# Expert weights loaded by two engines, half of each partition's run apiece

## What is computed

```
def expert_choice_ffn(h, w_router, w_gate, w_up, w_down):
    cap = EC_CAPACITY_FACTOR * n // N_EXPERTS              # 32 tokens
    aff = softmax(h @ w_router)
    g, idx = lax.top_k(aff.transpose(0, 2, 1), cap)
    xs = h[idx]
    a = jnp.einsum('becd,edf->becf', xs, w_gate)
    u = jnp.einsum('becd,edf->becf', xs, w_up)
    y = jnp.einsum('becf,efd->becd', jax.nn.silu(a) * u, w_down)
    y = y * g[..., None]
    return scatter_add(y, idx)
```

## Time and profile before

| | |
|---|---|
| median of three runs | 2280.72 us |
| the three runs | 2279.51, 2280.72, 2283.62 us |
| span of the profiled execution | 2283.8 us |
| PE busy | 1954.9 us, 86% |
| DVE, ACT, POOL busy | 929.5, 684.9, 4.1 us |
| bytes moved by DMA | 606.56 MB |
| chain that ended last, by engine | PE 52%, DMA 28%, DVE 13%, ACT 6%, issue 2% |

### The profile page before, as it was taken

One profiled execution on the slowest core, in us unless ns is written; L12 is line 12 of the kernel. 1 busy time (PEld: TensorE's weight loads), 2 busy tenths in 40 slices (PEclk: granted clock), 3 DMA queues, 4 the chain that ended last, 5 costly groups with the idle time before them and its releaser, 6 DMA issues.

```text
span 2283.8 us, 30557 instructions
## 1 busy us (share of the span) xinstructions
PE 1954.9 (86%) x13502; PEld 1393.4 (61%) x13502; DVE 929.5 (41%) x1596; ACT 684.9 (30%) x1090; POOL 4.1 (0%) x11
## 2 busy tenths in 40 slices
PE   7999999889898999999999888878889976566666
PEld 5589999878776999866774332324256843232323
DVE  5776655667665665664441010101065511010101
ACT  5345544553424454544422100000034310000000
POOL 0000000000000000000000000000000000000000
PEclk9999999899999999999999999999999988788878
DMA  6664445441457445512226999999932689999998
GB/s 262 239 263 154 169 162 188 156 167 56 185 221 281 167 148 181 206 41 111 111 111 287 428 427 428 428 427 428 428 137 111 260 355 426 428 427 427 427 427 339
DMA packets 44788, 606.56 MB, mean 266 GB/s; under 512 B 5104, under 2 KB 5232, under 8 KB 6768
## 3 DMA queue, kind: packets, MB, share of 16 engines
q1 hardware_dynamic: 43488, 597.61, 64.3%
q0 software_dynamic: 880, 4.98, 0.7%
q10 hardware_dynamic: 288, 2.02, 0.2%
HBM read 603.54 MB, written 1.05 MB: 265 GB/s over the span
## 4 chain that ended last, share of the span: by engine, by line
PE 52%; DMA 28%; DVE 13%; ACT 6%; issue 2%; SPq 0%; DVEq 0%; ACTq 0%
PE ps L85 51%; DMA m_more<-moe_up 10%; DMA m_ring<-moe_up 5%; DMA m_ring<-moe_down 3%; DVE m_WL L94 2%; DMA m_moe_sc<-moe_gate 2%; DMA m_side_slot<-moe_down 2%; DMA m_more<-moe_down 2%; DMA m_more<-moe_gate 1%; DMA m_ring<-moe_gate 1%; ACT m_WH L91 1%; ACT m_mix_sc L91 1%; DVE m_od_low L100 1%; DMA m_ring<-ev_in 1%; PE ps L88 1%
## 5 line engine op out<-in xcount | busy, mean ns | idle before, releaser
L94 DVE TENSOR_TENSOR m_WL<-m_ring,m_WH 128x1024 fp32r<-128x1024 f32 (+1 forms) x277 | 330.0, 1202 | 262.6 <-ACT m_WH L91 261.8
L85 PE MATMUL ps<-m_more,m_moe_sc 128*32 128x256 f32 (+1 forms) x1648 | 317.4, 538 | 80.6 <-DMA m_more<-moe_up 51.7
L91 ACT ACTIVATE m_WH<-m_ring 128x1024 fp32r<-128x1024 f32 (+1 forms) x277 | 282.4, 1034 | 132.2 <-PE ps L85 120.8
L85 PE MATMUL ps<-m_ring,m_moe_sc 128*32 128x256 f32 (+1 forms) x1104 | 244.8, 549 | 57.2 <-DMA m_ring<-moe_gate 28.3
L85 PEld LDWEIGHTS ps<-m_more,m_moe_sc 128*32 128x32 f32 (+1 forms) x1648 | 119.0, 141 | 226.7 <-issue 115.0
L85 PE MATMUL ps<-m_nH,m_WH 128*128 128x256 f32 x936 | 234.5, 287 | 18.3 <-ACT m_WH L91 18.3
L85 PE MATMUL ps<-m_nL,m_WH 128*128 128x256 f32 x936 | 234.5, 288 | 9.1 <-DVE m_nL L100 8.9
L85 PEld LDWEIGHTS ps<-m_nH,m_WH 128*128 128x128 f32 x936 | 181.0, 193 | 22.0 <-ACT m_WH L91 20.1
L85 PEld LDWEIGHTS ps<-m_nL,m_WH 128*128 128x128 f32 x936 | 181.1, 193 | 12.7 <-DVE m_nL L100 11.9
L85 PEld LDWEIGHTS ps<-m_ring,m_moe_sc 128*32 128x32 f32 (+1 forms) x1104 | 89.0, 143 | 149.8 <-issue 76.4
L91 ACT ACTIVATE m_moe_sc<-ps 32x512 f32<-32x512 f32 (+3 forms) x86 | 40.1, 472 | 385.9 <-PE ps L85 374.6
(11 more groups left out here) (307 smaller groups left out, 3199.2 us busy)
## 6 DMA issues: line engine op xcount, KB each, us to landing
m_more<-moe_up SPq DMA_DIRECT2D x37, 2048.0 KB, 26.6
m_more<-moe_gate SPq DMA_DIRECT2D x33, 2048.0 KB, 26.7
m_more<-moe_down SPq DMA_DIRECT2D x29, 2048.0 KB, 23.6
m_ring<-moe_gate SPq DMA_DIRECT2D x26, 2048.0 KB, 25.0
m_ring<-moe_down SPq DMA_DIRECT2D x25, 2048.0 KB, 26.7
m_ring<-ada SPq DMA_DIRECT2D x24, 2048.0 KB, 7.5
m_ring<-moe_up SPq DMA_DIRECT2D x22, 2048.0 KB, 25.6
m_ring<-ffn_down SPq DMA_DIRECT2D x16, 1408.0 KB, 6.0
```

The costliest lines, as they stand in the source:

```text
L85: return Issued() if self.dry else self.e.matmul(out, lhsT, rhs, start=start, stop=stop, skip_group_check=skip)
L91: return Issued() if self.dry else self.e.activation(*a, **k)
L94: return Issued() if self.dry else self.e.tensor_tensor(*a)
```

## The change

For the expert matrices alone (`moe_gate`, `moe_up`, `moe_down`), SP loads the left 8 KB of each partition's 16 KB (`width = SLOT // 2`, column tiles 0 and 1 of the chunk), and POOL the right 8 KB (column tiles 2 and 3). POOL goes through the same list of chunks in the same order, with the same events before each, once per layer and after its own load of `poolA`. Its loads signal semaphores of their own (`right0` to `right8`), and PE waits for both signals of a chunk where it waited for one. All other loads are as before.

```diff
+EXPERTS = ("moe_gate", "moe_up", "moe_down")
...
                             c = cc[h * nj // 4]
-                            pe.wait_ge(*at(("landed", c)))
+                            pe.wait_ge(*at(("landed", c))).wait_ge(*at(("right landed", c)))
...
                         c = down[h * nj // 4]
-                        pe.wait_ge(*at(("landed", c)))
+                        pe.wait_ge(*at(("landed", c))).wait_ge(*at(("right landed", c)))
...
         def pool_program():
             landed = {n: count(n) for n in ("p_landed", "ctx_landed", "dft_landed", "pools_landed")}
+            right = [count(f"right{i}") for i in range(9)]
...
                 pool.dma_start(wk[:, :], dr["poolA"]).then_inc(*landed["pools_landed"].mark(("poolA landed", l), by=16))
+                for n, (name, idx, j0, m, kt, _, slot, before) in enumerate(W.chunks):
+                    if name not in EXPERTS or idx[0] != l:
+                        continue
+                    for event in before:
+                        pool.wait_ge(*at(event))
+                    pool.dma_start(slots[slot][:, SLOT // 2:SLOT], dr[name][l][idx[1]][j0 // 4][:, SLOT // 2:SLOT]).then_inc(
+                        *right[slot].mark(("right landed", n), by=16))
...
                 per, width = TILES.get(kt, 1), m * kt * 128
+                if name in EXPERTS:
+                    width = SLOT // 2
                 sp.dma_start(slots[slot][:, 0:width], w[j0 // per][:, 0:width]).then_inc(*landed[slot].mark(("landed", n), by=16))
```

## The result

The changed kernel takes 2299.65 us (2298.78 to 2301.84, four runs), the kernel before 2281.38 us in the same comparison: a ratio of **1.0075** (95% interval 1.0062 to 1.0089), 14 to 20 us slower. It was forecast as slower, at 2290 us in a range of 2279 to 2304. The direction and the main mechanism held. The size was nearly double the forecast.

The account below looks back on a forecast made before the run. The prediction took DMA bytes over rate in the two expert parts as the bound. Rows (+40 ns) and signal (+12 ns) over 174 loads gave +9.0 us, other terms zero: 2290 us, range 2279 to 2304.

Parts of the forecast that it names:

- What bounds the kernel: Both expert parts: DMA engines full, shares 1.00 and 0.99, so bytes divided by rate bound them; PE has slack.
- Two of the signs: Expert parts: PE's load waits grow as much as the parts, some 4.5 us each; clearly later rights would be wrong.
- Part 1: Expert loads: twice as many rows, of 8 KB, cost +40 to +91 ns per 2 MB load; +40 taken.
- Part 2: Expert loads: a second signal for each load costs +12 ns (0 to 25) on each DMA engine.
- Part 3: POOL's issue of right halves: they start 0.3 us later, hidden by over 20 us of queued loads; zero.
- Part 4: PE's second wait per expert chunk: 0 to 0.04 us each, hidden in PE's slack except 0.04 us at the last load.
- Part 5: SP's and POOL's queues in the expert parts: equal turns with 8 KB rows mean equal bytes; zero.
- The sum: Whole kernel: 174 loads at +52 ns give +9.0 us, so 2290 us; at most +116 ns a load, +20 us.
- Two queues filling each other's gaps: Rival, expert parts: alternating queues reach 436 GB/s, -90 ns a load, -16 us, 2265 us; chance 0.07.
- The small cost: Rival, expert rows: fixed cost smaller than read, under 26 ns a load, -4 to +4.5 us, about 2283 us; chance 0.18.
- The right half falling behind: Rival, ends of expert parts: POOL gets fewer turns, last chunks bunch, +12 us, 2302 us with the +9; chance 0.08.
- POOL's loads one after the other, or descriptors late all the way: Rival, expert parts: right halves go at 5.1 us a load for 4.91, +33 us, 2314 us; chance 0.09.

Follow-up runs that it names:

- e9: Kernel before, expert matrices laid out by halves, so SP's one 2 MB transfer with one signal moves two 8 KB rows per partition; ratio 1.0052.
- e8: e1 with both half transfers on the slot's one semaphore, so PE waits once per chunk; ratio 1.0054 against the kernel before.
- e1: The change, but SP issues both halves of every expert chunk on one queue, a signal each; 2300.65 us, ratio 1.0069.
- e5: The change, but the last expert of each layer is loaded whole by SP; ratio 1.0050 against the kernel before.
- e2: Against the change: whole 2 MB expert chunks in 16 KB rows, first of each matrix by SP, second by POOL; ratio 1.0040.
- e7: Against e2: all expert chunks whole by POOL, all other weights by SP; ratio 1.0083.
- e6: e2, but the last expert of each layer is loaded by SP alone; ratio 0.9999 against the kernel before.

## Why the prediction was right, and where it was off

**What bounds the kernel.** Right. The DMA share stayed full, the rate fell from 428 to 421 GB/s (423 was forecast), and both expert parts grew. All that was found to change lies in them, but for 0.7 us less in the mixer between. Two of the signs came out otherwise: PE's waits for loads grew by 2.3 us in the first window (39.2 for 36.9), less than the part, and by 9.8 us in the second, and in the second part the rights land clearly later than the lefts.

**Part 1, the rows: the right term, mis-sized.** The bounds were +40 and +91 ns a load and I took +40, from 310.6 ns a row in a lone load of POOL. Measured: +71 ns (e9), 174 x 71 = 12.4 us, against 12.6 us in the parts. The step that failed is the price of a row from a lone load, and of its two windows the lower one. In the same measure, busy share over rows, e9's stream gives 101.1% of 3200 us / 10274 rows = 314.9 ns a row. The 313.8 ns that I put aside as an edge effect was nearer. But the measure itself isn't good enough: 16 x 314.9 less 8 x 616.3 is +108 ns, where the bytes moved give +71. Shares of 100.4 and 101.1% can't be exact, and 1% of a load is 49 ns, most of the effect. So whether a lone row is really faster than one in a stream can't be told from these numbers.

The estimate from the Trainium skill ("DMA: Bandwidth & Descriptors", Why small descriptors are slow), 3.5 ns a row, is too small here as the whole fixed cost of a row: the three row lengths give 9 ns.

**Part 2, the second signal.** Forecast +12 ns a load, 2 us. e8 has two transfers and two signals a load where e9 has one of each, and the same rows: 913.3 against 913.0 us for both parts, 0.3 us or 2 ns a load, and not surely more than nothing. This term was too high, which hid a part of the error in the first. There is a slip in the sum beside it: the 616.3 ns hold their share of the one signal of before, and the 310.6 ns hold none of the two of after. With both at the forecast's own 12 ns a load costs 64 and not 52 ns more, 11.1 us in all. Together the two were forecast at 9.0 us and are 12.9 us (e8's parts against before's).

**Part 3, where the loads are issued.** Wrong. I priced POOL's later start at 0.3 us, hidden behind 20 us of queue, from the landing times of two lone loads. Where both engines start from empty queues, POOL's first load lands a whole load late, and a deep queue doesn't hide a lag: in the second part it keeps it to the end.

**Part 4, the second wait.** Forecast at next to nothing, and it is: 0.3 us at most (e1 against e8). The reason given isn't quite right. After a landing the two waits take 0.1 us more than one (0.14 for 0.04 us), and little or none of that reaches the length of a part.

**Part 5, even turns.** Right, and shown for the software queue in full stretches: 5776 packets to 5776. But even turns don't give even halves when one side starts ahead. The change less e1 is what the lag costs: 1.7 us in the first part and 0.8 us in the second, **2.5 us**.

**The sum.** 12.6 (rows) + 0.3 (second transfer and signal) + 0.3 (wait) + 2.5 (lag) = 15.7 us in the two parts, less 0.7 in the mixer between, is the 15.0 of the table. The four terms are the steps from before to e9, e8, e1 and the change, so that they add up by construction. The check from outside is the rate for the first (12.4 us) and e5 for the last. The timed ratio says 17 us, 14 to 20. That 2299.65 us lie inside even the forecast's own bounds, 2286 to 2300 us, is in part luck: the upper bound pays 25 ns for a signal that costs 2, 4 us in all, and this covers the lag, which it had at nothing.

**The rivals.** Two queues filling each other's gaps: no, e1 on one queue and the change on two have the same 421 GB/s, as e2 on two has the 427 of whole rows. The small cost: no. The right half falling behind: it does, by a fraction of a load in the first part and by one in the second, at 2.5 us and not 12, on top of the forecast and not instead of it. It needs no uneven turns and no lag of more than two chunks, as I had thought. POOL's loads one after the other, or descriptors late all the way: no, e7 runs the second part on POOL's queue alone within 0.7 us of before.

## What to carry to other kernels

Where the DMA engines are full, count rows: a contiguous run per partition cost its bytes and about 9 ns of its engine's time here, at 16, 8 and 4 KB, so that a load's time grew with the number of runs, whoever issued them and in however many transfers. A second queue cost nothing in the middle of a stream. It cost at its ends, where the order between queues is lost: the loads that finish a stage shouldn't stand in another queue than those of the next stage. A queue that starts behind can stay behind as long as both are full. Seven slots, and nine, shared out between two queues left one of them a whole load behind (e2). To price a term of 1%, take it from bytes moved in a long window, not from the busy shares of a short one.

## What wasn't expected of the hardware

- The fixed cost of a row is the same at 16, 8 and 4 KB: 427.5, 421 and 409 GB/s, 9 ns a row.
- A software queue issued 0.46 us after a hardware queue landed its first 1 MB at 9.6 us against 4.8 us (19 packets to 188 in the window 1117 to 1123 us). In the second part the same lag, 4.9 us between landings, stayed while both queues were full; in the first it was 1.3 us.
- Two queues with loads of 64 partitions each move 246 GB/s with every DMA engine busy, and a 16 KB row takes 1070 ns.
- Three chunks of each layer's 96, moved from one queue to the other, decide 9 us (e2 against e6).
- The mixer that follows a part takes 166.5 to 168.9 us with the clock that TensorE is granted in 30 us of it, 1.00 to 0.89.
